# An encoder step on one core: the router starts before X is written, expert tables are spread, next weights load later, LayerNorm squares go to TensorE, and TensorE fills waits with unread products

## The reference, cut to what matters

```python
def _layer_norm(z, g, b):
    mu = jnp.mean(zf, -1, keepdims=True)
    var = jnp.mean(jnp.square(zf - mu), -1, keepdims=True)
    return ((zf - mu) * lax.rsqrt(var + LN_EPS) * g + b).astype(z.dtype)

def _hmoe(h, rg_w, rg_b, re_w, re_b, wg, wu, wd):
    gl = (xf @ rg_w + rg_b)
    gsel = jnp.argmax(gl, -1)
    ...
    top_v, top_i = lax.top_k(el_sel, TOP_K_INNER)
    top_w = jax.nn.softmax(top_v, -1) * gprob
    ...
    hid = jax.nn.silu(xf @ wg[e]) * (xf @ wu[e]) * comb
    return sum over e of hid @ wd[e]

def _trunk(...):
    for l in range(DEPTH):
        h = x * (1 + sc1) + sh1                      # sc, sh, gt: six vectors of adaLN, from c @ ada_w
        y = _rwkv7(h, ...) or attention over K, V
        x = _layer_norm(ALPHA * x + gt1 * y, ...)    # LayerNorm 0 (layer 0), 2 (layer 1)
        h = x * (1 + sc2) + sh2
        y = _hmoe(h, ...)
        x = _layer_norm(ALPHA * x + gt2 * y, ...)    # LayerNorm 1 (layer 0), 3 (layer 1)
```

## Time and profile before

| what | value |
|---|---|
| median of three runs | 1087.63 us (1087.05 to 1094.18) |
| the profiled execution: its own time | 1085.29 us |
| its span, first to last instruction | 1083.7 us |
| mean granted TensorE clock | 0.892 of full speed |
| TensorE products busy | 886.5 us, 82% of the span |
| VectorE, ScalarE, GpSimd busy | 336.0, 234.3, 173.7 us |
| moved by DMA | 230.47 MB, 213 GB/s on the mean |

### The profile page before, as it was taken

How to read it: one execution, slowest core, us unless ns; L and a number is a source line. 1 busy time by engine, 2 the same in 40 slices (tenths; PEclk the granted TensorE clock), 3 DMA queues, 4 the chain that set the end, 5 groups by cost and what they waited for, 6 DMA issues and landing times.

```text
span 1083.7 us, 19216 instructions
## 1 busy us (share of the span) xinstructions
PE 886.5 (82%) x8282; PEld 597.1 (55%) x8282; DVE 336.0 (31%) x849; ACT 234.3 (22%) x519; POOL 173.7 (16%) x216
## 2 busy tenths in 40 slices
PE   2799999899886877889875599898899778997742
PEld 0477667789764547545431377455367565454321
DVE  0522333445334544311112601231121542121126
ACT  0321225233212231111000423221222321110004
POOL 0100003020100032443111300000000234431122
PEclk9899989999997886899987699899899968999865
DMA  9642222330447501699997435355637315999831
GB/s 387 296 155 78 77 78 89 116 123 4 168 158 318 208 30 66 228 414 421 427 423 280 169 149 194 161 217 211 238 154 305 165 57 191 415 418 426 342 97 51
DMA packets 28997, 230.47 MB, mean 213 GB/s; under 512 B 7216, under 2 KB 7632, under 8 KB 14288
## 3 DMA queue, kind: packets, MB, share of 16 engines
q1 hardware_dynamic: 16704, 203.95, 46.7%
q0 software_dynamic: 8576, 15.83, 4.1%
q10 hardware_dynamic: 3632, 9.47, 2.6%
HBM read 223.21 MB, written 16.32 MB: 221 GB/s over the span
## 4 chain that ended last, share of the span: by engine, by line
PE 60%; DMA 21%; DVE 8%; issue 4%; ACT 2%; another core or an unknown queue 2%; SPq 1%; ACTq 1%; POOL 0%; DVEq 0%; POOLq 0%
PE ps L595 21%; DMA arena<-in_experts 8%; PE ps L919 8%; DMA arena<-in_w 8%; PE ps L721 5%; PE ps L616 4%; PE ps L930 3%; PE ps L728 3%; PE ps L904 3%; PE ps L582 3%; DMA ring<-in_w 2%; PE ps L1050 1%; DMA arena<-zbuf 1%; PE ps L734 1%
## 5 line engine op out<-in xcount | busy, mean ns | idle before, releaser
L595 PE MATMUL ps<-arena,ring 128*128 128x288 f32 x896 | 231.5, 421 | 13.8 <-DVE arena L1379 4.9
L595 PEld LDWEIGHTS ps<-arena,ring 128*128 128x128 f32 x896 | 173.8, 197 | 71.2 <-issue 16.9
L919 PE MATMUL ps<-arena 128*64 128x256 f32 x1152 | 149.9, 419 | 25.0 <-DMA arena<-in_experts 24.8
L919 PEld LDWEIGHTS ps<-arena 128*64 128x64 f32 x1152 | 87.9, 151 | 78.7 <-issue 27.4
L582 PE MATMUL ps<-con,arena 128*128 128x128 f32 (+3 forms) x254 | 52.5, 321 | 40.0 <-DVEq L1629 19.0
L582 PEld LDWEIGHTS ps<-con,arena 128*128 128x128 f32 (+3 forms) x254 | 32.1, 153 | 86.6 <-issue 37.8
L616 PE MATMUL ps<-arena,csil 128*32 128x512 f32 x256 | 40.8, 768 | 43.5 <-DMA arena<-in_w 42.4
L930 PE MATMUL ps<-arena 128*64 128x512 f32 x288 | 67.8, 593 | 1.6 <-DVE arena L1579 1.6
L1576 DVE TENSOR_TENSOR arena<-arena,ps 128x128 f32<-128x128 f32 x36 | 10.4, 288 | 184.2 <-ACT arena L1892 176.2
L721 PE MATMUL ps<-arena 64*64 64x64 f32 x1888 | 63.8, 221 | 4.5 <-issue 3.7
L721 PEld LDWEIGHTS ps<-arena 64*64 64x64 f32 x1888 | 60.7, 138 | 10.1 <-issue 8.4
(11 more groups left out here) (292 smaller groups left out, 1140.0 us busy)
## 6 DMA issues: line engine op xcount, KB each, us to landing
arena<-in_experts SPq DMA_DIRECT2D x32, 2048.0 KB
ring<-in_w SPq DMA_DIRECT2D x24, 2048.0 KB, 8.3
arena<-in_w SPq DMA_DIRECT2D x16, 2048.0 KB, 12.9
arena<-in_experts SPq DMA_DIRECT2D x32, 1024.0 KB
arena<-in_experts SPq DMA_DIRECT2D x4, 3072.0 KB, 19.4
arena<-zbuf ACTq DMA_DIRECT2D x8, 512.0 KB, 5.9
arena<-in_lora SPq DMA_DIRECT2D x1, 2560.0 KB, 40.5
hbuf<-arena ACTq DMA_DIRECT2D x4, 512.0 KB, 3.2
```

What stands on the lines that cost most here:

```text
L595: last = mm(ps[:, tile % 4, 0:T], wslot[j][:, k, o * P:(o + 1) * P], rhs_at(k), start=k == 0, stop=k == KT - 1)
L919: last = mm(ps[64 * j:64 * j + 64, 2 + b, 0:256], xselT[b][:, o:o + C], ewgu[slot][:, k, j * 256:(j + 1) * 256], start=k == 0, stop=k == K ...
```

## The change

It has seven parts. Numbers of lines behind "now" are those of the changed kernel.

1. **Router without the wait for X.** VectorE's wait for POOL's new X (`x_ready`) at the end of `layer_norm` goes; it now stands ahead of `select(0)`, since the selections `SEL` have moved to a part of `arena` that X's source still fills. The three memsets of the router move into the LayerNorm, ahead of the wait for the mean.
2. **Spread tables.** Of the four groups of table products two stay ahead of the expert loop; groups 2 and 3 come behind `step_u(0)` and `step_u(1)`. The copy to `TBL` is made once per group. The count of tokens (six records, L892) comes behind group 0.
3. **Late next weights.** SP issues the first half of `project(4)`'s weights when both halves of `zbuf` have been read, and not behind the last expert. All four pieces of adaLN turn 3 follow the second half, and TensorE works them off behind tiles 0 to 3 of `project(4)`. `fw` and the attention's first loads come later on POOL's queue.
4. **Squares on TensorE.** In LayerNorms 1 and 3 TensorE adds the eight squared tiles up itself, each as one product, between the transposes of stage 6; POOL adds up Z in VectorE's place.
5. **Centring is shared.** In all four LayerNorms VectorE centres tiles 0 to 4 and POOL tiles 5 to 7 (`OWN = 5`).
6. **Unread products.** `spin(bank, n)` issues n products of 128 x 288 whose results nobody reads: 14, 5 and 7 around the group norm, 6, 10 and 4 in each router, 14 behind each layer's experts, 5 ahead of `project(4)`.
7. Squares of LayerNorms 0 and 2 are written to another array (`SQB`).

```diff
+OWN = 5
...
-        SEL = [take(NTT * 4 * C) for _ in range(2)]
...
         hsil, hid, hidT = ([take(P) for _ in range(2)] for _ in range(3))
+        SEL = [take(NTT * 4 * C) for _ in range(2)]
...
             moe_loads(0)
+            for h in range(2):
+                sp.wait_ge(s[f"z_in{h}"], 48)
             half(4, 0)
-            sp.wait_ge(s["dn_mm"], NE)
-            for j in range(ADA_TURN - 1):
-                ada_weights(3, j)
-            sp.wait_ge(s["zsum"], 2)
             sp.wait_ge(s["o_over"], 2)
             half(4, 1)
-            ada_weights(3, ADA_TURN - 1)
+            for j in range(ADA_TURN):
+                ada_weights(3, j)
...
+            def spin(bank, n):
+                for _ in range(n):
+                    mm(ps[:, bank, 0:T], ident, con[:, 0:T], start=True, stop=True)
...
             pe.wait_ge(s["wkv_act"], ACT_TURN.all)
+            spin(5, 14)
...
             def layer_norm(n):
+                if n % 2:
+                    add_squares(n, KT - 2)
                 pe.wait_ge(s["ln_sum"], n + 1)
...
+                if not n % 2:
+                    pe.wait_ge(s["ln_ssum"], n // 2 + 1)
+                    mm(ps[:, 5, 0:T], co("mean"), ssum, start=True, stop=False)
+                add_squares(n, KT - 1).then_inc(s["ln_var"], 1)
+            def add_squares(n, k):
+                pe.wait_ge(s["ln_sq"], KT * n + k + 1)
+                return mm(ps[:, 5, 0:T], co("mean"), acts(SQB[n])[:, k, :], start=k == 0, stop=k == KT - 1)
...
+                spin(0, 10)
                 pe.wait_ge(s["mask_ready"], layer + 1)
...
+                tables(0)
+                for i, n in enumerate(TOK):
+                    last = mm(ps[:, 7, 448:464], ones[0:n, :], mask[0:n, i, :], start=i == 0, stop=i == 2)
+                last.then_inc(s["cnt_mm"], 1)
+                tables(1)
...
+                spin(1, 4)
                 step_t(0)
                 for e in range(NE):
                     if e + 1 < NE:
                         step_t(e + 1)
                     step_u(e)
+                    if e < 2:
+                        tables(2 + e)
...
-                if layer == 0:
-                    for j in range(ADA_TURN - 1):
-                        ada_slot(3, j)
+                spin(6, 14)
                 for k in range(KT):
...
                     last.then_inc(s["zt_mm"], 1)
+                    if k > 1:
+                        add_squares(2 * layer + 1, k - 2)
...
             def last_of_turn(tile):
-                if tile == 2:
-                    ada_slot(3, ADA_TURN - 1)
-                if tile == 3:
+                if tile < ADA_TURN:
+                    ada_slot(3, tile)
+                if tile == 4:
                     ada_columns(3)
+            spin(6, 5)
...
             def layer_norm(n):
                 Z, cent = acts(ZB[n]), []
+                if not n % 2:
+                    dve.wait_ge(s["ln_sq"], KT * n + 1)
+                    for x in (LG, RT, JI[n // 2][:]):
+                        did(V.memset(x, 0))
...
-                dve.wait_ge(s["x_ready"], KT * (n + 1))
...
+                dve.wait_ge(s["x_ready"], KT * (2 * layer + 1))
                 select(0)
                 select(1)
-                table(1, 0, 4)
+                table(0)
                 select(2)
+                table(1)
                 select(3)
...
             def layer_norm(n):
+                total, x, ready, done = (zsum_, Z, "z_ready", "ln_sum") if n % 2 else (ssum, Q, "ln_sq", "ln_ssum")
                 for k in range(1, KT - 1):
...
+                pool.wait_ge(s["ln_mu"], n + 1)
+                pool.wait_ge(s["ln_sq"], KT * (n + 1))
+                for k in range(OWN, KT):
+                    Pl.tensor_tensor(Z[:, k, :], Z[:, k, :], lnmu, ALU.subtract).then_inc(s["ln_cent"], 1)
```

77 lines of the change are left out of this document (37 added, 40 removed).

## The result

The changed kernel takes 1096.86 us (median of 20 runs, 1092.26 to 1104.07), the kernel before 1087.09 us in the same series. The ratio is 1.0077, with a 95% interval of 1.0058 to 1.0095. Forecast were 16 us less; it came out 10 us slower, outside the range. The profiled execution has a span of 1094.0 us, 10.3 more than that of before.

| stretch (us) | before | after | r9 | r14 | r16 |
|---|---|---|---|---|---|
| start to the end of the RWKV scan | 322.6 | 325.7 | 323.8 | 324.2 | 320.3 |
| to the first table product, layer 0 | 98.2 | 95.5 | 96.2 | 95.1 | 95.3 |
| to SP's second load of the loop | 30.2 | 36.0 | 29.5 | 26.6 | 25.9 |
| to the last scatter | 125.6 | 122.8 | 125.0 | 124.8 | 125.2 |
| to `project(4)` | 38.9 | 35.3 | 37.1 | 37.0 | 40.1 |

A forecast was written before the change was run, and what follows sets the result against it. DMA bounds the expert loops, so their start counts; elsewhere engine hand-offs and TensorE in project(4). Terms -2.3 -3.4 -3.0 -3.0 -3.0 -4.7 +5.6 -0.4 -0.4 -1.5 sum to -16.1 us, predicting 1071.5 us, range 1064 to 1082.

The forecast's parts named there:

- Item 3: Tables: spreading groups 2 and 3 behind gate-up products brings the expert loads sooner, -3.0 us in each layer.
- S + 27.1: Forecast time of SP's second load of the loop, S being the start of the first table product; before, S + 30.1.
- lower bound of -5.5: Tables: best case per layer, with groups 0 and 1 and the count fast as well.
- The first rival: Tables never go faster than at half the clock: +0.3 in place of -3.0, twice; 1078.1 us, chance 0.17.
- Item 1: Group norm: unread products fill TensorE's waits and hold the clock, -2.3 us.
- Item 2: Router up to the first selection: without the wait for X, -3.4 us in layer 0, -3.0 in layer 1.
- The third rival: Unread products meet half the clock and hold TensorE in router and group norm; slower, 1090.9 us, chance 0.04.
- Item 4: Late next weights: layer 0's last scatter -4.7 us, three more adaLN pieces inside project(4) +5.6 us.
- Item 5: LayerNorms 1 and 3: mean and variance at the full clock, less a centring loss, -0.4 us each.
- Item 6: Shared centring: VectorE's first two centrings beside POOL's lose 0.6 us once per LayerNorm, counted in other terms.
- Item 7: Into project(4): its first tile ends at 620.5 and not 622.0, -1.5 us.
- S + 17.5: Tables: forecast end of the first gate-up, after two groups, count, four unread products and transposes; S is first table product.

The follow-up runs named there:

- r9: Changed kernel with POOL's six job-table scatters taken out of its long row and issued behind expert 1's results; ratio to the kernel before 1.0003.
- r14: Changed kernel with the job-table scatters issued in pairs behind experts 1, 2 and 3, job list read at expert 8; ratio to the kernel before 0.9977.
- r16: Kernel before with only the router change, spread table groups 2 and 3, and job-table scatters in pairs; ratio to the kernel before 0.9919.
- r15: Kernel before with the router change, all table groups ahead of the loop, and job-table scatters in pairs; ratio to the kernel before 0.9997.
- r17: r16's kernel plus late next weights and all four adaLN pieces in project(4); ratio to the kernel before 0.9939.
- r8: Changed kernel with LayerNorms 1 and 3 as before, POOL adding squares and VectorE Z; ratio to the kernel before 1.0032.
- r7: Changed kernel with VectorE centring all eight tiles (OWN = 8); ratio to the kernel before 1.0038.
- r18: r16's kernel plus the unread products, those behind the loop in another bank; ratio to the kernel before 0.9928.
- r1: Changed kernel without any unread product; ratio to the kernel before 1.002.
- r4: Changed kernel with next weights and adaLN pieces of turn 3 ordered as before, unread products behind the loop in another bank; ratio to the kernel before 1.0047.
- r5: Changed kernel with SP's first load of each loop (2 MB) held back until the first down product; ratio to the kernel before 1.0181.
- r11: Kernel before with the router change, all table groups ahead, and job-table scatters issued behind expert 1's results; ratio to the kernel before 0.9977.
- r12: r11's kernel with table groups 2 and 3 behind the gate-ups of experts 0 and 1; ratio to the kernel before 0.9978.

## Why the prediction was wrong

**Item 3, the step that failed.** It was the path from the first gate-up to the second load. The forecast added up group 2, the transposes, a gate-up, group 3 and a down product and came to S + 27.1. The "9.4 to SP" of the kernel before holds more than its work: transposes, gate-up and down product are 6.1 us of it, 1.34 is an "issue" wait of TensorE, and SP issues the load 2.0 us after the down product has ended (449.01 and 450.99). I left these 3.3 us out of the sum of after, without saying what would remove them. They are what the path sees of ScalarE's long stop, which TensorE worked beside: its next gate-up and down product ran on. Nothing removed that stop, for it goes with POOL's row of indirect transfers, which begins at 436 to 438 us by the work of VectorE. In the changed kernel it hit TensorE itself: from the end of the first gate-up to the start of the second 8.5 us in place of 2.7, then 5.86 for that gate-up in place of 3.6. That is 8.1 of the 8.9 us that lie between S + 27.1 and S + 36.0. r9 shows the price with that row gone: group 2 and 3 in 2.01 us each (forecast 1.8), S + 29.5 with the unread products; and r16 S + 25.9. So 6.5 us are the row's. Of the 2.4 that are left 1.7 are the second gate-up, which the forecast had at the full clock (3.6 us) and which ran at a mean of 0.68 in r9; that is a second, smaller miss of the same sum. The mechanism of item 3, that products of three columns behind dense ones take less, was right (2.0 us a group and not 3.4), and its 3.0 us per layer were 3.5 in r16 against r15. Its lower bound of -5.5 was too near: groups 0 and 1 and the count at the full clock are another 3.3 and 0.7 by its own prices, -7.0. And the range's lower edge of 1064 takes the whole of both terms (1071.5 less 7.4) and not half of either; neither matters for this result, which lies on the other side. The first rival, that the tables never get faster, is refuted by the same rows.

**Where the 26 us went.** The forecast had 16.1 us less and the profile has 10.3 more. By the table, item 3 is 10.8 us of the 26.4 between them (+3.0 and +1.8 from S to the last scatter, and not -3.0 twice), items 1 and 2 are 5.2, the way from there into `project(4)` 1.5, `project(4)` itself 1.4, the last norm 0.5, and the two rows that move by themselves 7.0.

**Item 1, group norm: -2.3 forecast, -0.6 in the trace.** The 14 products took 7.06 us, as said, and L851, once L844, went from 5.84 to 4.15 us. But L836 still took 5.83, since TensorE stood idle for another 2.8 us and the clock fell; and `project(3)` goes by VectorE's tiles on its first product in any case, now at the full clock with a wait in front of each pair of records.

**Item 2, router: -3.4 and -3.0 forecast; -2.1 and -0.8 measured** (28.2 to 26.1, and 27.7 to 26.9). The wait for X did vanish and did nobody harm. The step that failed is "with six products in the gap ahead it stays fast". They ended 3.1 us before the first logits product, which waits for POOL's first part of h, and the logits then began at half the clock (0.53 in their first 3 us):

```profile
402.65 2.19 POOL arena L2116 x2
404.98 4.91 PE ps L884 x14
...
416.11 1.28 ACT L1914
```

The logits ended 2.2 us behind POOL, not 0.5, and all behind them, ScalarE's exponential too, came 1.5 us later than forecast, and some 2 in layer 1. The third rival (the ten unread products meet half the clock) did not happen: they took 5.0 us at a granted clock of 1.00. The granted clock stood at 1.00 behind 3 us of transposes, here as before: in the kernel before the last product that was no transpose ended at 407.3 us, the transposes at 411.0, and the clock was at 1.00 up to 415, while behind the six unread products, which ended at 400.7, it was at 0.53 from 404 to 407. So the trace speaks against the rule that I had named beside it (the Trainium skill, TensorE: Matmul & The Clock Gate, "Part 4: PE-mode transpose").

**Item 4, late weights: -4.7 + 5.6 forecast.** The terms were right in size: the scatter took 2.73 and not 7.93 us, and `project(4)` has three more pieces of 1.85. What failed is the step that a shorter scatter is a shorter path. Behind it POOL's job list and last gathers end last (5.99 and 5.86 us), and the late weights, issued from 592.79 us on, are in the queues with the gather: POOL waits 5.44 us for it to land, and 1.93 in the kernel before. To `project(4)` 3.6 us arrived here, 4.1 in r17.

**Item 5, LayerNorms 1 and 3: -0.4 forecast, about +0.4 in the traces** (r8 undoes it: 23.7 and not 24.1 us, 43.0 and not 43.5). **Item 6: 0.6 forecast, 0.7 in the trace of r7**, once per norm; the two collisions that the forecast drew from the Trainium skill (SBUF — State Buffer, "Who interferes with whom") would have been 1.2 us. **Item 7: -1.5 forecast, -0.6:** five unread products did not hold the clock over the 3.6 us in which TensorE then waited for X, and the first tile took 5.91 us and not 6.53 (in r16, without unread products, 5.95).

**The unread products** were costed by the waits that they fill. Four of them ahead of the first transposes fill no wait; in layer 0 they take 3.9 us at half the clock on the very path to the loads, and the load comes 3.7 us later for them (r18 against r16), in layer 1 0.1. My sum had them in S + 17.5 and never asked what the path would be without them.

So the slower result has one cause that is shown by the times and two that are shown in part. The burst that caught TensorE: taking it away gives 0.7% in r9 and 1.0% in r14. The unread products on the path: leaving them out gives 0.6% in r1, and 3.7 us in layer 0 of r18's trace, but r18's times (0.9928 against 0.9919) do not tell. The adaLN pieces that cost more than the scatter gives: by the traces alone, since r4 and r17 lie within the uncertainty. What makes the engines stop beside POOL's row stays open.

## What to carry to other kernels

A wait that stands in the chain of the kernel before must be carried into the sum of after by name, with what starts and ends it, or be removed by a named cause; a stall that hits one engine today hits the next one when work is moved into its place. Ask of each row of transfers on GpSimd who needs anything at that time, spread it, and keep gathers that a loop needs ahead of lists that only its end needs. A step that is moved from one side of a mark to the other (here the count) must be added to the gain on its new side before the gain is believed. No filler of this kernel is shown to have paid: leaving all of them out was faster (r1), and the four that stood in no wait cost their own 3.9 us in layer 0.

## What the runs showed of the hardware

While GpSimd issued seven to ten transfers in a row (about 1.3 us each), VectorE or ScalarE, and in some rows TensorE, stood still for 5 us and more on something the profile does not name, and went on between 1.6 us before the row's end and 1.8 us after it (40 rows of ten kernels). With the scatters issued in pairs, or behind expert 1, the stop behind the first gate-up was gone in r9 to r18, and holding back a 2 MB load did nothing (r5). Beside rows of four gathers VectorE was held up by 1.4 to 2.3 us in the changed kernel, r1 to r9, r11 and r12, and by 0.05 in r14 to r18. That it is the engines' next instructions that wait is my reading of "issue", and was not measured by itself; packets of the instruction queue begin at 445.4 us, 3 us before VectorE goes on, in r4, and at 447.3, 0.4 us before, in the changed kernel, so they don't settle it. The Trainium skill (Runtime: NRT & Kernel Launch, "Instruction fetch mechanics") says that each sequencer fetches the next 16 KiB of instructions over a DMA queue of its own while it executes, and that this is mostly hidden. The profile of the changed kernel has 67 packets with 1.10 MB in its instruction queue, 16 KB each, which agrees with the size; that it stays hidden does not hold here, if my reading is right.

The granted clock fell in the second gate-up of r9 and r18 (mean 0.68) though TensorE had worked since S with no pause of over 0.1 us, and stood at 1.00 in that of r14; no run shows why.

Table products of three columns took 0.071 us a record at half the clock and 0.042 at the full one (3.40 us for 48, 2.01 for 48).
